# Triangular inverse of a Gated DeltaNet chunk on 32x32 blocks in four row groups of TensorE

## The reference, cut to what matters

```
kk = k @ k.T                                    # 64 x 64
L  = strictly lower part of beta * kk * exp(g_i - g_j)
A  = I + L
U, W = solve(A, beta * v), solve(A, beta * exp(g) * k)
# scan over chunks:  delta = U - W @ S ;  o = (q exp g) @ S + Aqk @ delta ;  S = a S + k_dec.T @ delta
```

## Time and profile before

| | |
|---|---|
| median of 3 runs | 1989.32 us (1987.89, 1989.32, 7298.32) |
| the profiled execution | 1986.29 us |
| its span, first to last instruction | 1984.5 us |
| mean granted TensorE clock | 0.903 of full |
| mixing phase, first system product to last recurrence | 647.8 to 1112 us |
| busy in the span | PE 1663.6, PEld 1407.7, DVE 1010.5, ACT 661.3, POOL 548.6 us |

### The profile page before, as it was taken

How to read it: one execution, slowest core, us unless ns; L and a number is a source line. 1 busy time by engine, 2 the same in 40 slices (tenths; PEclk the granted TensorE clock), 3 DMA queues, 4 the chain that set the end, 5 groups by cost and what they waited for, 6 DMA issues and landing times. The chain is left out here.

```text
span 1984.5 us, 35548 instructions
## 1 busy us (share of the span) xinstructions
PE 1663.6 (84%) x15190; PEld 1407.7 (71%) x15190; DVE 1010.5 (51%) x1511; ACT 661.3 (33%) x995; POOL 548.6 (28%) x404
## 2 busy tenths in 40 slices
PE   4697787999996678888878579869999997999995
PEld 2685566689996677777777458647888876787784
DVE  3322333310110466666666665564454548767698
ACT  3227531532210222222222222345455543332333
POOL 1201100012111254445554331132223223403342
PEclk7578788999998898988989779979999998999998
DMA  6201312224554243223321333203444566343442
GB/s 278 68 32 48 96 62 69 67 90 139 165 173 130 74 125 87 87 87 87 87 87 56 112 130 104 85 21 133 159 148 144 164 236 219 111 165 115 147 159 85
DMA packets 168543, 229.83 MB, mean 116 GB/s; under 512 B 34189, under 2 KB 101121, under 8 KB 167362
## 3 DMA queue, kind: packets, MB, share of 16 engines
q1 hardware_dynamic: 161538, 205.79, 31.8%
q0 software_dynamic: 6848, 21.76, 3.4%
HBM read 165.78 MB, written 61.73 MB: 115 GB/s over the span
## 5 line engine op out<-in xcount | busy, mean ns | idle before, releaser
L87 PE MATMUL fps<-xh_m,w1r_hi 128*128 128x512 f32 x448 | 180.2, 402 | 26.9 <-issue 8.3
L87 PE MATMUL fps<-bh,ah 128*128 128x512 f32 x448 | 177.4, 396 | 28.4 <-issue 15.9
L88 PE MATMUL fps<-xl_m,w1r_hi 128*128 128x512 f32 x448 | 178.1, 397 | 0.0
L89 PE MATMUL fps<-xh_m,w1r_lo 128*128 128x512 f32 x448 | 178.0, 397 | 0.0
L88 PE MATMUL fps<-bl,ah 128*128 128x512 f32 x448 | 177.0, 395 | 0.0
L89 PE MATMUL fps<-bh,al 128*128 128x512 f32 x448 | 176.9, 395 | 0.0
L80 PE MATMUL ps_main<-whi,hhi 128*128 128x256 f32 (+1 forms) x496 | 149.9, 302 | 10.9 <-DVE wlo L620 10.9
L81 PE MATMUL ps_main<-wlo,hhi 128*128 128x256 f32 (+1 forms) x496 | 147.5, 297 | 0.0
L82 PE MATMUL ps_main<-whi,hlo 128*128 128x256 f32 (+1 forms) x496 | 147.3, 297 | 0.0
L80 PE MATMUL ps_main<-hhi,whi 128*128 128x512 f32 (+1 forms) x336 | 132.6, 395 | 0.0
L81 PE MATMUL ps_main<-hlo,whi 128*128 128x512 f32 (+1 forms) x336 | 127.9, 381 | 0.0
(11 more groups left out here) (311 smaller groups left out, 3796.7 us busy)
## 6 DMA issues: line engine op xcount, KB each, us to landing
s_hid<-hb SPq DMA_DIRECT2D x112, 256.0 KB, 2.3
araw<-s_hid SPq DMA_DIRECT2D x28, 1024.0 KB, 6.6
w1raw<-in_w_ff SPq DMA_DIRECT2D x16, 1024.0 KB, 6.4
w2b<-in_w_ff SPq DMA_DIRECT2D x16, 1024.0 KB, 5.0
raw<-in_w_in SPq DMA_DIRECT2D x14, 1024.0 KB, 5.3
wa<-in_w_ada SPq DMA_DIRECT2D x8, 1024.0 KB, 10.3
z_sb<-in_w_ada SPq DMA_DIRECT2D x16, 512.0 KB, 4.4
n_sb<-in_w_ada SPq DMA_DIRECT2D x16, 512.0 KB, 4.5
```

The source lines that it names most:

```text
L87: pe.matmul(out, lhi, rhi, start=start, stop=False, skip_group_check=True)
L88: pe.matmul(out, lhi, rlo, start=False, stop=False, skip_group_check=True)
L89: return pe.matmul(out, llo, rhi, start=False, stop=stop, skip_group_check=True)
```

## The change

The diagonal blocks of 32 are inverted first, all in tiles `[128, 4, 32]`: partition group g (32 partitions, g = 0 to 3) holds its own 32x32 block for each head. X and its transpose lie in one tile `xx` `[128, d, 2, 4, 32]`, so that one VectorE addition updates both. Every product of levels 1 to 4 becomes four 32x32 matmuls, one for each row group. The step from 32 to 64 is one block product (`lev == LAST`): Y on two row groups, no mask, the off-diagonal block of `tt` copied from PSUM by VectorE and one diagonal block by ScalarE (`keep_half`), the other through a product with the unit matrix. ScalarE fills `xx` with the unit matrix ahead of each step (`start_inverse`); level 0 is two products (`kkb` and its transpose) written under a mask (`copy_predicated`). The minus signs are gone since the row of beta is stored negated (three ScalarE copies for one). VectorE's `state(r, 0)` now stands ahead of `first_inverse(p)`. Two more masks are loaded and the level masks are a third as large.

The diff, cut (declarations of tiles, the NumPy masks and index helpers are left out):

```diff
             act.wait_ge(rt_ready, 1)
-            act.activation(rowt[:].rearrange("p x n -> p (x n)"), pg[1][:80, :384], ACT.Copy).then_inc(rt_out, 1)
+            for x, sign in enumerate((1.0, -1.0, 1.0)):
+                act.activation(rowt[:, x], pg[1][:80, x * P:(x + 1) * P], ACT.Copy, scale=sign).then_inc(rt_out, 1)
...
-            def first_inverse(s):
+            def start_inverse(s):
                 for d in R2:
-                    act.wait_ge(x0_ready[d], s + 1)
-                    act.activation(xs[:, d], cells(pd[d]), ACT.Copy).then_inc(x0_out[d], 1)
+                    after(act, pp_ready[d], LAST * s)
+                after(act, tt_half, 2 * s)
+                act.activation(xx[:].rearrange("p d z h j -> p (d z h) j"), eye[:].unsqueeze(1).broadcast_to([P, 4 * NH, H]),
+                               ACT.Copy).then_inc(eye_done, 1)
+
+            def keep_half(s):
+                for d in R2:
+                    act.wait_ge(x_done[d], LAST * (s + 1))
+                    after(act, tr_ready, 2 * s)
+                    act.activation(tt[:, d, :, d * H:(d + 1) * H], xx[:, d, 1], ACT.Copy,
+                                   scale=keep_m[:, d:d + 1]).then_inc(tt_half, 1)
...
             def first_inverse(s):
+                dve.wait_ge(eye_done, s + 1)
                 for d in R2:
-                    dve.wait_ge(kkb_done[d], s + 1)
-                    dve.tensor_tensor(xt[:, d], kkb[:, d], lev_m[:, 1 - d, 0].unsqueeze(1).broadcast_to([P, NH, C]),
-                                      ALU.mult).then_inc(x0m_done[d], 1)
-                for d in R2:
-                    dve.wait_ge(x0m_done[d], s + 1)
-                    dve.tensor_tensor(xt[:, d], eye[:].unsqueeze(1).broadcast_to([P, NH, C]), xt[:, d],
-                                      ALU.subtract).then_inc(x0t_done[d], 1)
+                    dve.wait_ge(x0_ready[d], s + 1)
+                    dve.copy_predicated(xx[:, d], first_m[:, d].bitcast(mybir.dt.uint32).unsqueeze(2).broadcast_to([P, 2, NH, H]),
+                                        pd[d][:, P:3 * P].rearrange("p (z h j) -> p z h j", z=2, h=NH)).then_inc(x_done[d], 1)
...
             def level_add(s, lev):
                 for d in R2:
                     dve.wait_ge(pp_ready[d], LAST * s + lev)
                     if lev < LAST:
-                        dve.tensor_tensor(xs[:, d], xs[:, d], cells(pd[d]), ALU.subtract).then_inc(x_done[d], 1)
-                    dve.tensor_tensor((xt if lev < LAST else tt)[:, d], xt[:, d], cells(pd[d], 1),
-                                      ALU.subtract).then_inc(xt_done[d], 1)
+                        x = xx[:, d].rearrange("p z h j -> p (z h j)")
+                        dve.tensor_tensor(x, x, pd[d][:, P:3 * P], ALU.add).then_inc(x_done[d], 1)
+                    else:
+                        dve.tensor_copy(tt[:, d, :, (1 - d) * H:(2 - d) * H], smalls(pd[d], 2)).then_inc(tt_done[d], 1)
...
             def first_inverse(s):
                 for d in R2:
-                    pe.wait_ge(x0t_done[d], s + 1)
+                    pe.wait_ge(kkb_done[d], s + 1)
                     if lat(s):
                         pe.wait_ge(at_done[d], s - TC + 1)
                     for h in range(NH):
-                        for c in R2:
-                            last = pe.matmul(pd[d][half(c), cell(h)], xt[half(c), d, h], eye[half(c)], start=True, stop=True)
+                        for g in range(4):
+                            a = kkb[rows32(g), d, h, inner(g)]
+                            pe.matmul(pd[d][rows32(g), small(h, 1)], a, eye[rows32(g)], start=True, stop=True)
+                    for h in range(NH):
+                        for g in range(4):
+                            a = kkb[rows32(g), d, h, inner(g)]
+                            last = pe.matmul(pd[d][rows32(g), small(h, 2)], eye[rows32(g)], a, start=True, stop=True)
                     last.then_inc(x0_ready[d], 1)
 
             def level_y(s, lev):
                 for d in R2:
-                    if lev == 1:
-                        pe.wait_ge(x0_out[d], s + 1)
-                    else:
-                        pe.wait_ge(x_done[d], (LAST - 1) * s + lev - 1)
-                        pe.wait_ge(xt_done[d], LAST * s + lev - 1)
+                    pe.wait_ge(x_done[d], LAST * s + lev)
                     for h in range(NH):
-                        for c in R2:
-                            last = pe.matmul(pd[d][half(c), cell(h)], kkb[half(c), d, h], xs[half(c), d, h], start=True, stop=True)
+                        if lev < LAST:
+                            for g in range(4):
+                                last = pe.matmul(pd[d][rows32(g), small(h)], kkb[rows32(g), d, h, inner(g)], xx[rows32(g), d, 0, h],
+                                                 start=True, stop=True)
+                        else:
+                            for c in R2:
+                                g, to = 2 * c + d, 2 * c + 1 - d
+                                last = pe.matmul(pd[d][rows32(to), small(h)], kkb[rows32(g), d, h, inner(to)], xx[rows32(g), d, 0, h],
+                                                 start=True, stop=True)
                     last.then_inc(y_ready[d], 1)
```

More of the change, by code:

```diff
@@ L848, in mix_phase @@
         att = [m.sb(f"att{b}", [P, 2, NH, C]) for b in R2]
-        xs, xt, ys, tt = (m.sb("gdn_" + n, [P, 2, NH, C]) for n in ("xs", "xt", "ys", "tt"))
+        xx, ys = m.sb("gdn_xx", [P, 2, 2, NH, H]), m.sb("gdn_ys", [P, 2, NH, H])
+        tt = m.sb("gdn_tt", [P, 2, NH, C])
         rr = m.sb("rr", [P, NH, P])
@@ L1346, in step @@
                     system(p)
+                if r is not None:
+                    state(r, 0)
+                if p is not None:
                     first_inverse(p)
                 if r is not None:
-                    state(r, 0)
                     residual(r, 1)
@@ L1406, in system @@
                 for d in R2:
-                    after(pe, xt_done[d], LAST * s)
+                    after(pe, tt_done[d], s)
                     for h in range(NH):
@@ L1444, in level_p @@
                     for h in range(NH):
-                        for c in R2:
+                        for g in range(4):
                             if lev < LAST:
-                                pe.matmul(pd[d][half(c), cell(h)], xt[half(c), d, h], ys[half(c), d, h], start=True, stop=True)
+                                pe.matmul(pd[d][rows32(g), small(h, 1)], xx[rows32(g), d, 1, h], ys[rows32(g), d, h], start=True, stop=True)
                     for h in range(NH):
-                        for c in R2:
-                            last = pe.matmul(pd[d][half(c), cell(h, 1)], ys[half(c), d, h], xt[half(c), d, h], start=True, stop=True)
+                        for g in range(4):
+                            if lev < LAST:
+                                to, y = g, ys[rows32(g), d, h]
+                            elif g % 2 != d:
+                                to, y = g - 1 + 2 * d, ys[rows32(g), d, h]
+                            else:
+                                continue
+                            last = pe.matmul(pd[d][rows32(to), small(h, 2)], y, xx[rows32(g), d, 1, h], start=True, stop=True)
+                    if lev == LAST:
+                        for h in range(NH):
+                            for c in R2:
+                                g = 2 * c + 1 - d
+                                last = pe.matmul(pd[d][rows32(g), small(h, 2)], eye[rows32(g)], xx[rows32(g), d, 1, h],
+                                                 start=True, stop=True)
                     last.then_inc(pp_ready[d], 1)
@@ L2747, in masks @@
     lev, smask = [], []
+    H = C // 2
+    q, e = (t % H)[:, None], np.arange(H)[None, :]
+    for h in (1, 2, 4, 8, 16):
+        block = q // (2 * h) == e // (2 * h)
+        up_q, up_e = q % (2 * h) >= h, e % (2 * h) >= h
+        lev.append(np.stack([block & up_q & ~up_e, block & ~up_q & up_e], 1))
+    first = np.stack([lev[0], lev[0][:, ::-1]], 2)
+    keep = np.stack([t // H % 2 == 0, t // H % 2 == 1], 1)
     for h in (1, 2, 4, 8, 16, 32):
@@ L2760, in masks @@
     return {"k_ident": np.eye(P, dtype=np.float32), "k_sel": f32(sel), "k_tri": f32(tri), "k_trix": f32(trix),
[L2761 to L2762 removed]
+            "k_chunk": f32(chunk), "k_inc": f32(inc), "k_eye": f32(q == e), "k_keep": f32(keep), "k_first": f32(first),
+            "k_lev": f32(np.stack(lev[1:], 2)), "k_smask": f32(np.stack(smask, 1))}
 class Kept:
```

36 lines of the change are left out of this document (24 added, 12 removed).

## The result

The changed kernel takes 2029.48 us (median of 4 runs, 2027.26 to 2030.93) against 1988.61 for the kernel before on the same chip: ratio 1.0208, 95% interval 1.0188 to 1.0228. One run of the kernel before took 7298 us; the ratio leaves it out. I had forecast 1961 us and a range up to 2010. The profiled execution has a span of 2025.5 us, 41.0 more than before.

What follows compares the result with a forecast made beforehand. No engine was full; the inverse was a chain swinging between VectorE and TensorE. Latent steps -20, context steps -9 and mask loads +1 gave -28 us on 1986.3, 1958, plus 3.0 for the median: 1961 us, range 1928 to 2010.

Steps and rivals of the forecast that it cites:

- r: Start-to-start time of two TensorE records in the inverse: 29 ns before, taken as 10 ns; 5.8 us for each ns.
- rival C: Every product of the inverse: records start no sooner than 25 to 29 ns apart on average; +70, 2059 us; chance 0.11.
- Rival D: TensorE's instruction supply: 40 more packets of 16 KB could stop it in the stage; +19 to +75 us; chance 0.06.
- hard form: Instruction supply in the stage: each of 40 more packets brings a stop of TensorE; +75, 2036 us.
- mild one: Instruction supply in the stage: one in four of 40 more packets brings a stop of TensorE; +19 us.
- The clock: TensorE in the latent stretch: a mean clock well below 0.91 would take back part of the gain; no size given.
- b: Level 1 of the inverse in a latent step, behind recurrence work: shorter first and second products, -0.85 us.
- d: Level 2 in a latent step: mask, products, updates and next first product shorter, -1.16 us.
- f: Level 3's updates and level 4's first product in a latent step bring the keys' transpose and scores forward, -0.8 us.
- g: Level 5's first product in a latent step, -0.4 us; its last copies lie beside the state products.
- term (h): Switches between tile shapes in a latent step: ten added at 0.17 us, six uncovered, +1.0 us.
- Rival E: TensorE's saving turns into waits for GpSimd and the accumulations, only context steps gain; 1975 us; chance 0.12.

Runs made afterwards that it cites:

- e2: The change, but VectorE turns X's 32x32 blocks to make its transpose in place of TensorE's products; 1971.97 us, ratio 0.9909 to the kernel before.
- e4: The change with the moving side of level 1 to 4 products 64 columns wide for three of four heads, same records; 2021.93 us, ratio 1.0154 to the kernel before.
- e1: The kernel before with seven runs of small unused products put ahead of the mixing loop; 32x32 products measured 27 ns a record over groups of 128.
- e8: The kernel before with level 1 to 4 products moving 32 of their 64 columns, same records; 2033.08 us, ratio 1.0222 to the kernel before.
- e12: The kernel before plus 26 unused filler products in TensorE's waits in each latent step; 1979.36 us, ratio 0.9947 to the kernel before.

## Why the prediction was wrong

- **The record, r.** Taken as 10 ns. In bursts it is 11.4 ns on average at the full clock (128 records of the start, the first at 890.93 and the last at 892.38 of the trace after) and 13.4 at the low one. That was about right, with some luck: the burst that I read it from was seven records, and the 21 records around it (1076.77 to 1077.20 of the trace before) lie 21 ns apart. The failed step was to use a burst's pace as a rate that lasts: over packets it is 27 ns, rival C's figure. Its floor for each record is not there; its remark that bursts may only be a queue emptying was close to what happens. By the rule of the Trainium skill, TensorE: Matmul & The Clock Gate, section "Wait — 56ns, not 53.3ns?", no record starts sooner than 25 ns after another; the runs contradict it inside a group (11.4 and 13.4) and give nearly its number across groups, from supply.
- **Rival D** named the right mechanism, place and count: 40 packets more, 43 stops. I gave it 0.06 and said that one packet in four would stop TensorE; its stops came to 50 us, between the 75 of its hard form and the 19 of its mild one. That the hard form's 2036 us is near the 2029 is in part luck, as the clock is not in it. In the trace before, the shortest distance of two instruction packets was already 3.37 us, and 128 records at 10 ns, with their loads one packet, take 1.3 us: a lone level of 192 records with as many loads needs one and a half packets, so would take 5.2 us, not 2.64 (an estimate from these distances). Measured, the first three levels of context step 0 take 6.2 to 6.4 us from first product to first product, against 3.5 to 4.1 before. The context steps, costed at -9, cost +18. I had looked at the packets' bytes and not at their distance.
- **The clock** was costed at nothing in the sum and named only as something that might take back part. This term, put at nothing, is the second step that failed: TensorE's other records take 5.9 us more in a latent step, against the forecast saving of 2.5. Of my sum, the parts that shorten TensorE's products (b, d, f, g) were real in kind: 3.6 us a step.
- **Mode switches**, term (h): changes of tile form in the stage go from 130 to 203 and take 0.12 to 0.20 us at the full clock, up to 0.35 at the low one, from start to start. 73 more, where I counted some 100; the 0.17 us that I had priced lies in the range at the full clock.
- **Rival E**, waits for GpSimd: TensorE's wait for the weighted keys (L1069 before, L1076 after) rose from 15.5 to 18.6 us over eight steps. As forecast it did not decide.
- **A slip in the sum**: the four parts of term (d) add up to -1.26 us and not -1.16; it moves the forecast by 1 us and decides nothing.

## What to carry to other kernels

Before splitting products into smaller tiles, count records, loads included, in the densest stretch, and hold them against the shortest distance of instruction packets in the trace (here 256 records with loads per 3.4 us). And read the granted clock: a product made shorter can slow everything else on TensorE by more than it saves. Where VectorE works on 32x32 blocks anyway, it can turn them itself for 0.31 us per 128 values in each partition (e2), which spared 3200 records; those cost 63 us here.

## What the runs showed of the hardware

- Instruction packets of 16 KB start no sooner than 3.3 us after one another in any of these traces (3.30 in e4). Where records are short, TensorE stops for the next one: 27 ns a record over a long run, 13.4 within a packet (e1).
- 64x64 tiles on two row groups take 29.2 ns a record whether 32 or 64 columns move, at the full clock; halving the columns saves nothing there (e1), and in a kernel it cost 44 us (e8).
- Four row groups of 32 that write one PSUM bank, each its own 32 partitions, do overlap: 13.4 ns a record, where one 32x32 tile by itself takes 53 at the same low clock (e1, L1419). The Trainium skill, TensorEngine Tiling (Array Packing), "Gotcha 1: PSUM Pressure", says that different row tiles cannot access one bank simultaneously; a quarter of the time of one tile contradicts it.
- Useless products in TensorE's waits made the otherwise unchanged kernel before 0.5% faster (e12).
